# A decoder layer on eight cores: another order of work at the start, in the middle and at the end

## What is computed

```python
h = rmsnorm(r, g_mix)
proj = h @ w_in                              # 1024 -> u | B | C | h, 512 each
y_pool = ((trailing mean of u over 2/4/8/16 rows) - u) @ w_pool * scale
y_conv = B * causal_dwconv(C * h)            # width 3
r = r + concat(y_pool, y_conv) @ w_out
h2 = rmsnorm(r, g_ffn)
a, v = split(causal_dwconv(h2 @ w_up))       # 1024 -> 5632, width 3
r = r + (silu(a) * v) @ w_down               # 2816 -> 1024
r = r + sigmoid(rmsnorm(r, g_ple) @ w_ple_gate) * (p @ w_ple_proj)
y = rmsnorm(r, g_final)
```

## Time and profile before

| | |
|---|---|
| median of 3 runs | 840.49 us (840.45 to 881.43) |
| profiled execution | 840.07 us |
| span of its slowest core (core 5) | 838.5 us |
| spans of the other cores | 835.0 to 837.7 us |
| TensorE busy | 802.4 us (96%), 4180 matmuls |
| VectorE, ScalarE, GpSimd busy | 564.9, 350.5, 231.7 us |
| moved | 129.33 MB, mean 154 GB/s |

### The profile page before, as it was taken

One profiled execution on the slowest core, in us unless ns is written; L12 is line 12 of the kernel. 1 busy time (PEld: TensorE's weight loads), 2 busy tenths in 40 slices (PEclk: granted clock), 3 DMA queues, 4 the chain that ended last, 5 costly groups with the idle time before them and its releaser, 6 DMA issues.

```text
span 838.5 us, 13292 instructions; the slowest of 8 cores (835.0 to 838.5 us)
## 1 busy us (share of the span) xinstructions
PE 802.4 (96%) x4180; PEld 784.4 (94%) x4180; DVE 564.9 (67%) x848; ACT 350.5 (42%) x575; POOL 231.7 (28%) x329
## 2 busy tenths in 40 slices
PE   3899999999999999999999999989999999999993
PEld 2799999999999999999999999989999999999993
DVE  3478746877655774577664967775796886677566
ACT  2523334545203552455446545214552142355463
POOL 2110102163412442244402011211255154244200
PEclk9999999999999999999999999999999999999997
DMA  8853342354362326233346228681485947555625
GB/s 227 249 169 120 101 139 81 121 158 143 107 228 83 94 76 197 81 126 101 116 137 170 73 80 263 217 257 49 153 231 181 352 129 194 183 178 175 174 68 188
DMA packets 36163, 129.33 MB, mean 154 GB/s; under 512 B 4224, under 2 KB 6912, under 8 KB 35328
## 3 DMA queue, kind: packets, MB, share of 16 engines
q0 software_dynamic: 30880, 107.26, 42.3%
q1 hardware_dynamic: 4784, 20.25, 7.2%
q10 hardware_dynamic: 432, 0.97, 0.4%
HBM read 119.44 MB, written 9.88 MB: 154 GB/s over the span
## 4 chain that ended last, share of the span: by engine, by line
PE 92%; DVE 3%; ACT 2%; issue 1%; DMA 1%; DVEq 0%; SPq 0%; ACTq 0%
PE PS L317 92%; DVE SCR L175 1%; DMA R<-xT 1%; DVE R L175 1%; DVE SCR L172 1%; ACT RS L169 0%; ACT SCR L169 0%; ACT L169 0%; DVE H L175 0%; ACT GB L169 0%; DVE GB L175 0%; DVEq L1035 0%; DVEq L1031 0%; DVE R L172 0%; ACT H L169 0%
## 5 line engine op out<-in xcount | busy, mean ns | idle before, releaser
L317 PE MATMUL PS<-H,WS 128*128 128x418 f32 (+5 forms) x2720 | 531.2, 353 | 8.0 <-DVE H L175 7.8
L317 PEld LDWEIGHTS PS<-H,WS 128*128 128x128 f32 x2720 | 510.4, 189 | 19.3 <-issue 12.6
L175 DVE SCALAR_TENSOR_TENSOR SCR<-PS,VEC,SCR 128x832 f32<-128x832 f32 (+3 forms) x288 | 247.4, 873 | 73.5 <-ACT SCR L169 55.9
L317 PE MATMUL PS<-GB,WS 128*128 128x416 f32 (+1 forms) x1280 | 255.7, 351 | 5.2 <-DVE R L172 2.2
L317 PEld LDWEIGHTS PS<-GB,WS 128*128 128x128 f32 x1280 | 239.4, 189 | 8.8 <-issue 7.3
L284 POOL DMA_DIRECT2D WS<-wst x204 | 111.2, 548 | 274.7 <-PE PS L317 251.4
L169 ACT ACTIVATE SCR<-PS,VEC 128x832 f32<-128x832 f32 (+3 forms) x144 | 125.4, 876 | 116.5 <-PE PS L317 116.1
L172 POOL TENSOR_TENSOR GB<-SCR 128x832 fp32r<-128x832 f32 (+3 forms) x72 | 112.2, 1559 | 205.5 <-DVE SCR L175 189.4
L172 DVE TENSOR_TENSOR R<-PS,R 128x416 f32<-128x416 f32 (+3 forms) x128 | 84.5, 691 | 67.3 <-PE PS L317 66.9
L175 DVE SCALAR_TENSOR_TENSOR H<-R,VEC,RS 128x416 fp32r<-128x416 f32 (+1 forms) x112 | 67.3, 643 | 47.9 <-ACT RS L169 47.9
L169 ACT ACTIVATE H<-R 128x416 fp32r<-128x416 f32 (+1 forms) x98 | 50.4, 547 | 67.9 <-DVE R L172 61.9
(11 more groups left out here) (49 smaller groups left out, 192.7 us busy)
## 6 DMA issues: line engine op xcount, KB each, us to landing
WS<-wst POOLq DMA_DIRECT2D x188, 512.0 KB, 5.2
yT<-R SPq DMA_DIRECT2D x4, 1664.0 KB, 7.3
WS<-wst POOLq DMA_DIRECT2D x16, 384.0 KB, 3.7
R<-xT SPq DMA_DIRECT2D x2, 1664.0 KB, 10.2
R<-xT SPq DMA_DIRECT2D x3, 832.0 KB, 11.0
GB<-pT POOLq DMA_DIRECT2D x5, 416.0 KB, 3.7
R<-xT SPq DMA_DIRECT2D x4, 416.0 KB, 8.8
SCR<-xT SPq DMA_DIRECT2D x1, 1664.0 KB, 13.3
```

The source lines that it names most:

```text
L175: P.op("dve", (lambda e: e.scalar_tensor_tensor(out=out, in0=in0, scalar=scalar, in1=in1, op0=op0, op1=op1)), r=r, w=w)
L317: ins = e.matmul(o, l, m, start=st, stop=sp)
```

## The change

Five edits, all in the order and place of instructions:

1. The constants VEC are loaded first on GpSimd's queue, and all four pieces of block 0's x on SyncE's queue (ScalarE's queue had two of them, and VEC).
2. `warm(n)` issues n matmuls of 128 columns whose result nobody reads, into a bank of the ring: 4, 4, 4 and 18 within block 0's norm, and 28 between block 1's statistics and its root.
3. In the second tile `fill` takes five steps instead of four behind units j = 0 to 2, and one instead of none behind each unit of j = 3.
4. Of block 3's eight output applies, two each now belong to groups 2 to 4 and one each to groups 5 and 6 of the last gate block (before: two each to groups 3 to 6). The table for Ln and Exp is loaded within the last group, ahead of the last two squares. The three small outputs are issued before the gate blocks.
5. The last four transfers hold 3, 2, 2 and 1 channel groups instead of 2 each.

```diff
+        def warm(n):
+            b = banks(1)
+            pe_run([(PS[:, b, 0:128], ONES[:, :], ONES[:, :], True, True)] * n, ["ONES"], [("ps", b)])
...
-        for q, eng in enumerate(("sp", "act", "sp", "act")):
-            x_in(0, q, 2 * q, 2 * q + 2, eng=eng)
-        P.dma("act", "semC", lambda e: e.dma_start(out=VEC[:, :], in_=vec_d), w=["VEC"])
+        P.dma("pool", "semC", lambda e: e.dma_start(out=VEC[:, :], in_=vec_d), w=["VEC"])
+        for q in range(4):
+            x_in(0, q, 2 * q, 2 * q + 2)
...
+                if final:
+                    act(DUMMY[:, 1:2], EPSV[:, 0:1], AF.Ln, r=["EPSV"], w=["DUMMY"])
...
             n0.square(k)
             n0.mm()
+            if k % 2:
+                warm(4 if k < 7 else 18)
...
                     if nm:
+                        warm(28)
                         nm.finish()
...
-                    nf = (1, 0, 2) if t == 0 else ((1, 0, 4) if j < 3 else (0, 0, 0))
+                    nf = (1, 0, 2) if t == 0 else ((1, 0, 5) if j < 3 else (0, 0, 1))
...
+            if lastt:
+                out_dma(u_out_d, UOUT[:, :, :], ["UOUT"])
+                out_dma(c_out_d, COUT[:, :, :], ["COUT"])
+                out_dma(f_out_d, FOUT[:, :, :], ["FOUT"])
...
-                        for i in range(3, 7):
+                        for i in (2, 3, 4):
                             md[i].append(q.pop(0))
                             hk[i].append(q.pop(0))
+                        for i in (5, 6):
+                            md[i].append(q.pop(0))
...
-                for q in range(4):
-                    for k in (2 * q, 2 * q + 1):
+                for q, (k0, k1) in enumerate(((0, 3), (3, 5), (5, 7), (7, 8))):
+                    for k in range(k0, k1):
                         apply_y(fin, k)
```

More of the change, by code:

```diff
@@ L741, in gate_block @@
             for oc in range(8):
+                final = b == LASTB and oc == 7
                 bg = banks(1)
@@ L955, in build_program, with out_dma @@
                 prev = nm
+            if lastt:
+                def out_dma(dst, src, r):
+                    P.dma("sp", "semO", (lambda e: e.dma_start(out=dst, in_=src)), r=r)
+                out_dma(u_out_d, UOUT[:, :, :], ["UOUT"])
+                out_dma(c_out_d, COUT[:, :, :], ["COUT"])
+                out_dma(f_out_d, FOUT[:, :, :], ["FOUT"])
             gu, pu = [], []
@@ L1009, in build_program @@
             else:
-                act(DUMMY[:, 1:2], EPSV[:, 0:1], AF.Ln, r=["EPSV"], w=["DUMMY"])
                 fin.square(7)
-                def out_dma(dst, src, r):
-                    P.dma("sp", "semO", (lambda e: e.dma_start(out=dst, in_=src)), r=r)
-                out_dma(u_out_d, UOUT[:, :, :], ["UOUT"])
-                out_dma(c_out_d, COUT[:, :, :], ["COUT"])
-                out_dma(f_out_d, FOUT[:, :, :], ["FOUT"])
                 fin.finish()
-                for q in range(4):
-                    for k in (2 * q, 2 * q + 1):
+                b = fin.b
+                for q, (k0, k1) in enumerate(((0, 3), (3, 5), (5, 7), (7, 8))):
+                    for k in range(k0, k1):
                         apply_y(fin, k)
-                    b = fin.b
-                    P.dma("sp", "semYL%d" % q, (lambda e, q=q, b=b: e.dma_start(
-                        out=yT[b, :, 2 * q:2 * q + 2, :], in_=R[:, RSLOT[b], 2 * q:2 * q + 2, :])),
-                        r=[rkey(b, 2 * q), rkey(b, 2 * q + 1)])
+                    P.dma("sp", "semYL%d" % q, (lambda e, k0=k0, k1=k1: e.dma_start(
+                        out=yT[b, :, k0:k1, :], in_=R[:, RSLOT[b], k0:k1, :])),
+                        r=[rkey(b, k) for k in range(k0, k1)])
         assert ust["next"] == nunits
```

## The result

| | before | with the change |
|---|---|---|
| first comparison, median | 840.62 us (840.45 to 881.43, 4 runs) | 855.76 us (855.63 to 856.05, 4 runs) |
| ratio | | 1.0181 [1.0161, 1.0201] |
| profiled execution and slowest span | 840.07 and 838.5 us (core 5) | 855.85 and 854.3 us (core 4) |
| TensorE busy, matmuls | 802.4 us, 4180 | 826.8 us, 4238 |

The forecast of 833.5 us and its range of 829.5 to 838.0 missed. Two later comparisons gave the same program 0.9979 [0.9967, 0.9990] and 0.9976 [0.9966, 0.9986], about 838 us. So two things have to be explained: 17 us that come and go, and 4.5 us between 838 and 833.5 that are always there.

The account below looks back on a forecast made before the run. The chain of waits was 92% matmul, so only start, middle stalls, tail and low-clock stretches could give time. Core 5's terms summed to -7.7 us; core 3's -6.0 gave 831.5, with offsets 833.5 us, range 829.5 to 838.

Parts of the forecast that it names:

- (C): Rival: unread matmuls overrun before the first projection and block 1; up to 842.8 us, chance 0.05; milder overrun 836.3, chance 0.07.
- Transfers and start (-3.5): Start to block 1: earlier x and weights start TensorE at 15.0 us; gain 3.5 us, the first 2.2 included.
- rival (A): At the start, weights issued 2 us sooner collide with the last pieces of x: 836.0 us, chance 0.18.
- With the clock up: From the first projection TensorE follows the applies at 0.19 us per matmul, first half done at 19.4 us.
- Unread matmuls (+0.2 and 0): Short matmuls at 90 ns: the 28 before block 1 cost 0.2 us, the 18 before the first projection 0.
- 36p: Overrun at the start: 18 + 4 unread matmuls at low-clock price p and 28 at p/2, against about 8 us cover.
- Clock held from 28 to 36 us (-1.7): Behind the stall before block 1, the 28 hold the clock up, sparing core 5 half its low stretch: -1.7 us.
- Bank ring (+0.9): First tile, part 2's first down projection near 310 us: TensorE waits for shifted PSUM banks, +0.9 us.
- Pooling sums ahead (-1.2 and -1.6): Middle, near 556 to 566 us: one 1.8 us stall replaces two, -1.2 us, and the clock holds, -1.6 us.
- below both: Middle: the new 1.8 us stall is shorter than earlier stalls of 2.31 and 2.23 us, so the clock holds.
- Rival (B): Unread matmuls don't hold the clock, or it falls behind the middle stall: 835.1 to 835.8 us, chance 0.20.
- Tail (-0.8): Last applies and transfers: earlier table load and smaller last piece, -0.8 us, 0.45 of it by the first apply.

Follow-up runs that it names:

- d_after: The change itself, unaltered, run again beside the kernel before: 837.74 to 838.27 us, ratio 0.9979.
- fourth comparison: The change again and three variants (d_ring, d_no18, d_nopool) against the kernel before at 839.82 us; the change took 837.74 to 838.27 us.
- d_ring: The change with unread matmuls that leave the ring of banks where it was, against the kernel before: 837.27 to 837.54 us, ratio 0.9972.
- b_28: The kernel before with only the 28 unread matmuls added, against the kernel before: 838.56 us, ratio 0.9982.
- a_nowarm: The change without any unread matmuls, against the kernel before: 836.84 us, ratio 0.9964.
- a_only28: The change without the 4, 4, 4 and 18 unread matmuls, keeping the 28, against the kernel before: 836.80 us, ratio 0.9965.
- d_no18: The change without the 18 unread matmuls, keeping 4, 4, 4 and 28, against the kernel before: 835.92 us, ratio 0.9953.
- d_nopool: The change without unread matmuls and with the pooling sums in their old place, against the kernel before: 837.35 us, ratio 0.9972.
- e_no18: The same program as d_no18, run again against the kernel before: 836.02 us, ratio 0.9956.
- e_best: The change without the 4, 4, 4 and 18 unread matmuls and with 20 instead of 28, against the kernel before: 835.64 us, ratio 0.9950.
- a_no28: The change without the 28 unread matmuls, keeping 4, 4, 4 and 18, against the kernel before: 836.86 us, ratio 0.9966.
- f_kout3: e_best with three banks instead of four in the first step of block 3's output projection, against the kernel before: 837.57 us, ratio 0.9973.
- f_split: f_kout3 with block 4's remaining pooling steps moved behind the first three residual adds, against the kernel before: 833.20 us, ratio 0.9925.
- e_big18: The change with one group of 30 unread matmuls in place of 4, 4, 4 and 18, against the kernel before: 839.64 us, ratio 0.9998.
- e_after: The change itself, run once more against the kernel before: 837.96 us, ratio 0.9976.
- third comparison: The change and three variants on a chip where every kernel ran at a lower clock: 889.28 to 891.47 us, the kernel before 894.54 us.

## Why the prediction was wrong, step by step

Landmarks of core 5, before (838.5 us) and in the profile of the change without the stretch (`d_after`, 836.3 us):

| | before | change | moved | forecast | moved, mean of eight cores |
|---|---|---|---|---|---|
| block 1's first projection | 30.46 | 30.14 | -0.3 | -3.3 | +1.0 |
| first down projection of part 2 | 310.18 | 308.76 | -1.1 more | -0.8 more | -0.4 more |
| `PS<-GB,WS` behind the middle | 636.69 | 634.64 | -0.6 more | -2.8 more | -0.8 more |
| end | 838.5 | 836.3 | -0.1 more | -0.8 more | -0.7 more |
| sum | | | -2.2 | -7.7 | -0.9 |

The last column is there because core 5 was the latest core before: on it the start looks better, and the tail worse, than on the others. The slowest core of eight sets the time, and its block 1 starts at 30.66 us before and at 30.77 with the change.

That the later 838 us nearly lie in the range is luck: the range reached there for the overrun of (C), and what happened is several smaller misses.

**The clock held down (17 us, not in the sum).** The first comparison's miss is this and nothing else: outside it the changed kernel is faster than before. The prediction knew two levels of the clock and had no case for a third, and no rival held it. Did the change bring it? The counts: in the first comparison all four executions of the change had it, on six to eight cores, and the kernel before, at 840.45 to 840.76 us in three of its four, did not; later, stretched pairs came in 4 of 10 and 0 of 9 executions of the change, against 1 of 22 and 0 of 21 of the kernel before beside them. That 4 of the 5 executions with a pair that these two kernels had in the fourth comparison fall to the change's 10 of 32 would happen by chance about 1 time in 40. `d_ring` had one in 7, `b_28` one in 12, and the other kernels without the 18 (`a_nowarm`, `a_only28`, `d_no18`, `d_nopool`, `e_no18`, `e_best`) none in 36, nor had `a_no28` in 5 and `f_kout3` and `f_split` in 17. So it seems to come more readily with all the unread matmuls, in some comparisons and not in others; each ran on another chip and at another time, which the runs don't separate. That the unbroken start brings it was argued and not shown: `e_big18` and `e_after` speak against it, and which part does, or whether it was the chip's state alone in the first comparison, stays open.

**Transfers and start (-3.5): mostly wrong.** The weights are issued 2 us sooner on every core, and on core 5 the rest came as forecast: `d_no18` starts its first projection at 14.98, forecast 15.0. But before, only four of the cores were so late; the others began it at 14.2 to 14.8 us. On the mean of the eight cores the first projection moves from 15.6 to 15.2 in `d_no18`, and the first apply goes back, from 14.0 to 14.2 (14.3 in `d_after`), where -0.5 was forecast. That is the mark of rival (A), the last pieces of x coming later, in a small measure (the eighth square ends at 11.4 us instead of 11.1); that the weights hold it up is likely and not shown.

Block 1 starts at 28.44 on core 5 of `d_no18`, -2.0 instead of -3.3: 0.6 of the difference is the price of the 28, and the rest lies in the block ahead, which ends at 25.4 instead of 24.6. I had taken all eight statistics matmuls at 0.19 us. Four of them stand 0.44 us apart, at the pace of ScalarE's squares, which come only behind its copies of block 0's u:

```profile
20.76 2.75 ACT L169 ACTIVATE H<-R 128x416 fp32r<-128x416 f32 x6
...
21.46 1.74 PE L322 MATMUL PS<-H,ONES 128*128 128x416 f32 x4
```

"With the clock up" failed too: it came up at 18.0 to 20.7 us in `d_no18` and at 18.0 to 21.5 in `d_after`, 2 to 5.4 us behind the first projection, and the later it rises the later block 1 starts (28.4 us on core 4 of `d_no18`, 29.8 on core 1).

**Unread matmuls (+0.2 and 0): the price and the cover failed.** I priced a short one at 90 ns, near a share of its columns. It takes 111 ns at the high clock, and at the low clock 213 ns where I had 120 to 150. (The 0.42 us that rival (C) gives a full statistics matmul at the low clock is a busy time; from start to start it is 0.35.) The 28 so take 3.1 us against a wait of 2.3, and the 18, which I covered with the wait for the weights, stood ahead of a projection whose weights now came sooner: the change itself had removed the cover. The page "TensorE: Matmul & The Clock Gate" of the Trainium skill, section "Back-to-back issue gap", gives 81 ns for this width; by the trace it is 111. This is rival (C)'s mechanism in its mild form, which had 0.07: at p = 0.21 us its 36p is 7.7 us, inside the 8 us of cover that I had counted, and yet the 18 alone cost 1.2 us at block 1 on the mean of the eight cores.

**Clock held from 28 to 36 us (-1.7): right,** on every core, with 28 or with 20. The size fits what a low stretch costs in the middle, 1.6 us (7.71 against 6.15 us for the same 32 matmuls).

**Bank ring (+0.9): right,** an idle time of 0.72 us that costs 0.95 from start to start, removed by `d_ring`. What I missed is the stall near 411 us, which this same term could have removed.

**Pooling sums ahead (-1.2 and -1.6): wrong.** One stall is left of two, as forecast, but it is 2.48 us and not 1.8. The product ended 0.7 us later than worked out, since ScalarE's copy for j = 3 now waits for the `SCR` buffer of the chain that was pulled ahead: I followed VectorE's order and not the buffers that it hands on. With 2.48 us the argument that 1.8 was "below both" fell too, and seven of eight cores show the low level behind it, so the 1.6 us aren't gained. Rival (B)'s second half holds.

**Tail (-0.8): mostly wrong on core 5, about right on the others.** A stall in the last gate block grew, because two of block 3's applies now stand there in VectorE's stream. Before, then with the change (`d_after`), core 5, TensorE:

```profile
807.05 1.73 PE L317 MATMUL PS<-H,WS 128*128 128x408 f32 x8 [1.38 <-DVE H L175]
```
```profile
805.33 1.72 PE L322 MATMUL PS<-H,WS 128*128 128x408 f32 x8 [1.72 <-DVE H L175]
```

That is 0.34 us lost. From TensorE's last two matmuls on weights to the end of the span 0.47 us are gained (15.58 us on core 5 before, from 822.92; 15.11 on core 4 in the first comparison, from 839.19; 15.12 on core 5 of `d_after`). But core 5's tail was the shortest of the eight before. On their mean it goes from 15.96 to 14.95 us: 1.0 gained, 0.35 of it ahead of the first apply, forecast 0.45, and 0.67 in the last pieces, forecast 0.35. Less the 0.34 that makes -0.7.

## What to carry to other kernels

A filler for an idle stretch has to be priced at the clock it will run at, and against the idle stretch that the same change leaves, not the one in the old trace; a filler that is too short costs little, one that is too long delays everything behind it. When steps are pulled ahead on one engine, follow the buffers they hold back from the other engines, and when a stall moves with the bank it waits for, look for the engine whose backlog is behind both: moving the last pooling steps behind three residual adds brought 4.4 us against `f_kout3`, where the bank edit alone had done harm, and with both edits 0.9925 stands against the 0.9950 of `e_best`, 2.1 us over two chips. A transfer order that helps the latest core can hold back the others, so look at all eight. And read the row of the granted clock first: a ratio of 1.018 that four executions agreed on was 2% off in two later comparisons, and that row says why before any theory of the program does.

## What the runs showed of the hardware

- TensorE's granted clock has a third level here, 0.81 of full speed. It came as one stretch of 160 us per core in the first comparison, equally long on the two cores of each neighbouring pair, and as many of about 15 us in the third; by their mean clock single pairs had it in the fourth. It went away with TensorE still 100% busy.
- A matmul of 128 columns with its own weight load takes 111 ns at 2.4 GHz and 213 ns at 1.2 GHz, against 190 and 347 ns for one of 416: less than a third of the columns costs about 60% of the time. At the level of 0.81 one of 416 takes 213 ns (core 4 of the first comparison).
- Short matmuls on a matrix of ones did not raise the clock. On core 4 TensorE was busy from 9.06 us on without a break that the timeline shows, and the projections from 16.72 us stood 360 ns apart until 21.2 us; on core 5 of `d_no18`, where it stood 2.5 us before 14.98 us, they came down to 196 ns at 18.2. The same matmuls kept the clock where it was over a wait of 2.3 us, on all cores of all twelve profiles that have them outside the third comparison (nine kernels, 20 or 28 of them); without them it fell on 3 to 8 of the eight cores (`d_nopool` 3, before 4, `a_nowarm` 6, `a_no28` 8).
- Stalls of the same 2.48 us were followed by the low level on some cores and not on others, from one of eight to all eight; one of 0.90 us (`f_split`) on none, one of 3.4 us (`f_kout3`) on all eight.
